# Two gathered u rows behind each batch of one-hots instead of three, the rest later

## What is computed

```python
q = (ht @ w_query).reshape(PEER_BLOCK, PEER_HEADS, PEER_QDIM)
s1 = jnp.einsum('thd,hkd->thk', q[..., :PEER_HALF], keys1)
s2 = jnp.einsum('thd,hkd->thk', q[..., PEER_HALF:], keys2)
...                                   # top 16 of the sums: expert (t, 8 heads, 16), top_s
g = jax.nn.softmax(top_s, axis=-1)
act = jax.nn.gelu(jnp.einsum('thkd,td->thk', u_tab[expert], ht))
return jnp.einsum('thk,thkd->td', g * act, v_tab[expert])
```

## Time and profile before

| | us |
|---|---|
| median of three runs | 1619.41 (1616.14 to 1623.07) |
| the profiled execution | 1620.23 |
| its span | 1618.4 |

### The profile page before, as it was taken

One profiled execution on the slowest core, in us unless ns is written; L12 is line 12 of the kernel. 1 busy time (PEld: TensorE's weight loads), 2 busy tenths in 40 slices (PEclk: granted clock), 3 DMA queues, 4 the chain that ended last, 5 costly groups with the idle time before them and its releaser, 6 DMA issues.

```text
span 1618.4 us, 21748 instructions
## 1 busy us (share of the span) xinstructions
PE 1525.7 (94%) x7951; PEld 1268.7 (78%) x7951; DVE 1269.3 (78%) x2000; ACT 688.2 (43%) x1273; POOL 996.8 (62%) x608
## 2 busy tenths in 40 slices
PE   6996997978999999999999999999999999999996
PEld 2344575437889999999999998998888888788875
DVE  6768741283889999969887897549989888999997
ACT  2030464204233433358877876344333333333332
POOL 3511000023326777776766887788978888889875
PEclk9997999989999999999999999999999999999998
DMA  9974205412306787778898999999999999999971
GB/s 367 327 216 53 30 1 186 165 52 87 122 27 206 258 277 278 269 266 326 335 361 345 355 376 346 417 333 378 376 379 362 376 376 382 383 370 383 372 267 65
DMA packets 217302, 438.91 MB, mean 271 GB/s; under 512 B 37220, under 2 KB 129892, under 8 KB 215404
## 3 DMA queue, kind: packets, MB, share of 16 engines
q1 hardware_dynamic: 179612, 302.44, 53.2%
q0 software_dynamic: 36864, 134.23, 22.6%
q10 hardware_dynamic: 720, 0.85, 0.2%
HBM read 379.66 MB, written 56.64 MB: 270 GB/s over the span
## 4 chain that ended last, share of the span: by engine, by line
PE 26%; DMA 21%; issue 8%; DVE 8%; ACT 7%; POOL 4%; SPq 2%; POOLq 0%; ACTq 0%; DVEq 0%
DMA u_raw<-in_peer_uT 9%; DMA a_in<-act_scr 7%; DMA v_raw<-in_peer_v 6%; PE ps L1649 5%; PE ps L1650 5%; PE ps L1651 5%; ACT hot1h L1582 3%; POOL vl L1541 3%; DVE ps L1745 2%; PE ps L1327 2%; PE ps L1328 2%; PE ps L1329 2%; DVE w_f L1853 2%; DVE wl L1858 1%; ACT stage L1590 1%
## 5 line engine op out<-in xcount | busy, mean ns | idle before, releaser
L1535 POOL TENSOR_TENSOR utl<-u_raw,uth 128x1024 fp32r<-128x1024 f32 x128 | 307.2, 2401 | 150.3 <-ACT uth L1554 148.9
L1649 PE MATMUL ps<-h2h,uth 128*128 128x384 f32 x1024 | 348.2, 340 | 3.1 <-POOL utl L1535 3.1
L1541 POOL TENSOR_TENSOR vl<-v_raw,vh 128x1024 fp32r<-128x1024 f32 x128 | 311.5, 2435 | 52.4 <-ACT vh L1554 50.4
L1651 PE MATMUL ps<-h2h,utl 128*128 128x384 f32 x1024 | 343.2, 335 | 0.0
L1650 PE MATMUL ps<-h2l,uth 128*128 128x384 f32 x1024 | 342.9, 335 | 0.0
L1672 PE MATMUL ps<-vh,wh 128*128 128x512 f32 x768 | 300.0, 391 | 2.8 <-DVE wl L1858 2.6
L1673 PE MATMUL ps<-vl,wh 128*128 128x512 f32 x768 | 298.9, 389 | 0.0
L1674 PE MATMUL ps<-vh,wl 128*128 128x512 f32 x768 | 298.9, 389 | 0.0
L1853 DVE TENSOR_TENSOR w_f<-a_in,g_in 128x384 f32<-128x384 f32 x128 | 213.0, 1664 | 51.7 <-DMA a_in<-act_scr 50.7
L1554 ACT ACTIVATE vh<-v_raw 128x1024 fp32r<-128x1024 f32 x128 | 135.3, 1057 | 205.9 <-DMA v_raw<-in_peer_v 165.6
L1649 PEld LDWEIGHTS ps<-h2h,uth 128*128 128x128 f32 x1024 | 192.9, 188 | 3.8 <-POOL utl L1535 3.0
(11 more groups left out here) (357 smaller groups left out, 2338.5 us busy)
## 6 DMA issues: line engine op xcount, KB each, us to landing
u_raw<-in_peer_uT SPq DMA_DIRECT2D x128, 512.0 KB
v_raw<-in_peer_v SPq DMA_DIRECT2D x128, 512.0 KB
w_ada<-in_w_ada SPq DMA_DIRECT2D x12, 2048.0 KB, 14.6
act_scr<-acts SPq DMA_DIRECT2D x64, 384.0 KB
g_scr<-stage SPq DMA_DIRECT2D x12, 2048.0 KB
g_in<-g_scr SPq DMA_DIRECT2D x32, 768.0 KB
a_in<-act_scr SPq DMA_DIRECT2D x64, 384.0 KB
w_q<-in_peer_w_query SPq DMA_DIRECT2D x8, 1024.0 KB, 5.4
```

Of the source, the lines that this page charges most:

```text
L1535: tt(k.utl[b % 3][:, :, :].rearrange(f3), k.u_raw[:, b % 4].rearrange(f3), k.uth[b % 3][:, :, :].bitcast(F32).rearrange(f3), ALU.subtract) ...
L1541: tt(k.vl[:, n % 4], k.v_raw[:, n % 4], k.vh[:, n % 4].bitcast(F32), ALU.subtract).then_inc(k.vl_done, 1)
L1649: mm(o, hi, k.h2h[:, kt, SP:T], start=(kt == 0), stop=False)
L1651: ins = mm(o, lo, k.h2h[:, kt, SP:T], start=False, stop=(kt == DK - 1))
```

## The change

Of the u rows, two instead of three follow each batch of one-hots (33 to 80), 25 instead of 23 follow behind the last batch (81 to 105), and the remaining 22 are used in v blocks 1 to 11, two in each (106 to 127). The v rows begin in v block 15 instead of 6, at six in five blocks instead of eight in seven; the last is used in v block 121 and fetched in 115. The gelu of the dots moves to v block 14. `row_steps()` moves the fetches: u rows 81 to 112 go behind u blocks 109 to 127, 113 to 127 behind v blocks 0 to 8, and the v rows begin at v block 11. No operation and no transfer is added or removed.

```diff
--- before.py
+++ after.py
@@ -1378,12 +1378,12 @@
     for j in range(2 * SLOTS):
         if j < 33:
             at = 8 + 1.3 * j
-        elif j < 105:
-            at = 53 + (j - 33) * 0.777
+        elif j < 81:
+            at = 53 + (j - 33) * 1.166
         elif j < SLOTS:
-            at = 109 + (j - 105) * 0.5
+            at = 109 + (j - 81) * 0.6
         else:
-            at = NBLK + 1 + (j - SLOTS) * 0.875
+            at = NBLK + 11 + (j - SLOTS) * 0.82
         steps[int(at)].append(j)
     return steps
 
@@ -1422,7 +1422,7 @@
         for half in range(2):
             HOT1H_AT.setdefault(block_of(PER_BATCH * m) - 2 + half, []).append((m, half))
     LAST4 = NBLK - 4
-    SP_GELU, SP_WEIGH = 4, 6
+    DOTS_END, SP_GELU, SP_WEIGH = 13, 14, 15
     f3 = "p k n -> p (k n)"
     BANK = dict(zip([(t, half) for t in range(DT) for half in range(2)], (4, 5, 6, 7, 2, 3)))
     y_sp = ps[:, 0:2].rearrange("p a n -> p (a n)")
@@ -1898,19 +1898,21 @@
         step(ins)
         for m in range(NBATCH):
             hots(m)
-            use_rows(3)
-        use_rows(SLOTS - done["rows"])
+            use_rows(2)
+        use_rows(25)
 
         weight(0)
         for n in range(1, NBLK):
             weight(n)
             split_w_low(n - 1)
-            if n == SP_WEIGH:
+            if n < DOTS_END:
+                use_rows(min(2, SLOTS - done["rows"]))
+            elif n == SP_WEIGH:
                 dve.wait_ge(k.gelu_sp, 1)
                 tt(k.w_sp[:, :], k.w_sp[:, :], k.gate_sp[:, :], ALU.mult).then_inc(k.w_sp_ready, 1)
                 dve.wait_ge(k.w_sp_ready, 1)
             if n >= SP_WEIGH:
-                use_rows(min(SLOTS, (n - SP_WEIGH + 1) * 8 // 7) + SLOTS - done["rows"])
+                use_rows(min(SLOTS, (n - SP_WEIGH + 1) * 6 // 5) + SLOTS - done["rows"])
             if n == NBLK - 3:
                 dve.wait_ge(k.row_used, 2 * SLOTS)
                 dve.wait_ge(s_gate2, 16)
```

## The result

The changed kernel takes 1635.66 us (median of 4 runs, 1632.86 to 1638.73) against 1619.48 for the kernel before (4 runs). The ratio is 1.0088, interval 1.0057 to 1.0119: 9 to 19 us slower. The forecast was 1621.5 and "within 0.5%" at 0.50. The measured time is 14 us above the forecast and outside the range that the sum gave itself (1614 to 1629). It lies inside the whole range only because that reached to rival B, which stood at 1636.

What follows compares the result with a forecast made beforehand. TensorE was taken as nearly full, DMA as the second full resource, with 18 us at most to win. Terms -7 - 3 + 5 + 7 = +2 us on 1620.2 gave 1622.2, forecast 1621.5 after allowing for the median; range 1610 to 1636.

Steps and rivals of the forecast that it cites:

- rival B: v blocks 11 to 115: DMA gives only 374 GB/s whatever is asked; +16 us, 1636; chance 0.27.
- Part 1: Beside the one-hots, 48 rows instead of 72 relieve the DMA and cut waits on `stage`: -7 us, bounds 3 and 9.4.
- Part 2: Last u blocks, 109 to 127: slightly fewer rows in 109 to 119 shorten the `u_raw` load: -3 us, bounds 0 and 6.
- Part 3: Hand-over and v blocks 0 to 8: gathers delay `a_in`, fetches slow GpSimd: +5 us, bounds 1 and 9.
- VectorE's two dots hide: v blocks 1 to 11: two dots a block cost VectorE 2.6 us but overlap its port wait behind GpSimd's `vl`.
- Rival D: v blocks 1 to 11: the dots don't hide, VectorE needs 5.2 us a block; 1630; chance 0.06.
- Part 4: v blocks 11 to 115: rows at 1.22 a block ask more than the DMA serves: +7 us, bounds 0 and 13.
- Part 5: The rest: later gelu of the dots and last v row in block 121 are covered by leads; nothing counted.
- C: v blocks: DMA can give more than the 372 GB/s asked; -10 us, 1610; chance 0.17.
- A: Whole kernel: DMA time is moved, not saved; 1621.5 us, own range 1614 to 1629; chance 0.50.

Runs made afterwards that it cites:

- e1: Kernel before with two u rows behind each batch of one-hots and the 24 freed rows left out, neither gathered nor multiplied: 1607.59 us, 0.9922 of before.
- e7: Changed kernel with the gelu of u block 127 first and the last 22 u rows left out, gather and dot: 1614.10 us, 0.9954 of before.
- e8: Changed kernel with the gelu of u block 127 first; last 22 u rows not gathered, their dots made on an old buffer: 1620.65 us, 0.9988 of before.
- e9: Kernel before with v rows from block 15 at six in five blocks and the gelu of u block 127 first: 1625.45 us, 1.0017 of before.
- e2: Changed kernel with three u rows again behind each one-hot batch, one behind the last; 22 u rows and v rows placed as changed: 1631.04 us, 1.0076 of before.
- c4: Kernel before with v rows still from block 6 but at 14 in 13 blocks, last used in block 124: 1616.91 us, 0.9983 of before.
- e4: Changed kernel with the gelu of u block 127 ahead of the high parts of v blocks 2 and 3: 1632.72 us, 1.0076 of before.
- e3: Kernel before with only its v rows moved, from block 15 at six in five blocks: 1628.43 us, 1.0051 of before.
- c1: Kernel before with v rows at 14 in 13 blocks and u rows nine before, 64 after, 22 behind the one-hots: 1638.52 us, 1.0097 of before.

## Why the prediction was right or wrong

- *The time*: the sum gave +2 us, and the kernels differ by 14 by the ratio and 16 by the medians. The upper end of the range, 1636, was 0.3 us above the measured median; that it holds the result is luck as far as the sum goes, since it was put there for rival B.
- *What bounds the kernel*: right in the main. DMA time is short from the one-hots on, and each stage moved the way the rows of that stage said. That no more than 18 us were to be won held for every version. But the 18 counted waits, and in v blocks 12 to 122 the kernel before lost 5.2 us where the waits said 2.6.
- *Part 1, -7*: right, -8.0, and -7.5 in e1. The mark (waits on `stage` of 1 to 4 us) was met with 2.4. The share fell to 0.86, not 0.80.
- *Part 2, -3*: the size was off, -1.3. The longest `u_raw` fell from 17.67 to 13.90 us, as said, and the clock held. But with rows up to the hand-over the `utl` came just in time, and TensorE waited 2.0 us for it in three waits.
- *Part 3, +5, bounds 1 and 9*: this term was mis-sized, +12.6. Its mechanism was in the text (gathers beside the hand-over, late `a_in`, waits on `wl`); e7 and e8 show that the gathers make all of it. I took 5 us more for the landing, 12.7 in all, and it took 14.9. What I left out: SP itself is held at the issue (7.22 us), so the tiles after the first come later still; the weights of blocks 2 and 3 and the last gelu hang on the second `a_in`, not the first; and the clock at 1.2 GHz behind a stop of 6.7 us costs 1.6 us more. I priced one landing and looked at one consumer. GpSimd, for which part of the 5 us stood, never made TensorE wait: none of its waits there was on `vl`.
- *"VectorE's two dots hide"*: wrong. They hide in time, since TensorE lost nothing in e8's blocks 0 to 12 beyond 0.6 us, but not in the lead: 4.41 us a block against 4.08. Rival D saw the cause, put 5.2 us on such a block, and had the wrong place for the loss; it is paid after block 12.
- *Part 4, +7*: +10.1, inside its bounds, but for another reason. The rate by itself is worth 2.1 us against before (e9) where I counted 6.4. The rest I read as lead lost before block 12 (a `w_f` begins 7.0 us ahead of that block, 12.4 before), for which my 7 held 0.6 us and the upper bound 4. The dots can take that much: e8 against e7, with the same rate, is 7.9 us by the stages and 5.5 us by the ratios (0.0034 x 1620). But they needn't: e2 has the same dots and the same v half, and loses only 3.0 us in blocks 12 to 122. It has fewer gathers ahead of the v blocks. What share of the changed kernel's lost lead is the dots' and what the late tiles' is not shown.
- *Part 5, nothing*: right, 24.6 us from block 122 to the end in every kernel.
- *The chances*: rival B had the time (1636) and 0.27. Its condition, a served rate under about 377, was just missed: 378 and 377 were served in the changed kernel and 383 in c4. So B was right in its number and its sign and not in its mechanism. C's premise held in that the DMA can give more than 376, but its sign was wrong: that doesn't help when the asking engines are late. A, the sum, had the mechanism of the first two parts and missed its own range by 7 us.
- The parts add up to +13.5 us by the stages; the spans differ by 12.7, since the u blocks of the changed kernel's execution began 0.9 us earlier.

Still open: why the first `a_in` held SP for 7.22 us. The profile names a landing of an earlier store as what ended it, but the program waits there only for the store of u blocks 0 and 1, which had long landed. Without the last 22 rows the same issue took 2.60 us (e7) and 2.29 (e8), in e4 4.10; no experiment took that apart. And whether 22 rows at one a block in the first v blocks would have kept the lead was not tried, since the v rows can't begin before all dots are done.

## What to carry to other kernels

Moving work out of a crowded stage gains only what the target stage has to spare, and the spare is counted in the lead of the buffers, not in the waits of the bottleneck engine: here 24 rows gave 8 us where they left, and cost 23 where they arrived, together with the v rows that had to begin later for them. Before blaming the longest stop of a trace, move the thing it waits for; if another wait takes its place, the cause lies further up. And look for the other direction too: spreading the v rows over seven more blocks, two lines, gained 0.2% where the whole change lost 0.9%.

## What the runs showed that I had not expected

- An engine that is 8% too slow for eleven blocks, with 0.6 us lost by TensorE there, costs 5 to 8 us in the hundred blocks after, because loads are only asked for when it frees a buffer (e8: DMA share 0.64 and 0.72; e7: 0.76 and 0.99).
- Taking the gathers away from GpSimd can slow VectorE: with `vl` back to back, four `w_f` and `wl` in a row took 2.6 us each, where before only two of the four did (e3), and it took a change in ScalarE's order to hide it (e9).
- The waits on `stage` don't fall with the rows one by one: 9.4, 8.7, 8.5 and 2.4 us with 72, 64, 60 and 48 rows.
- At 1.077 rows a v block blocks 12 to 122 take 448.8 us with no wait (c1 to c4), at 1.143 454.0 and 453.1 with waits (before, e1), and at 1.22 456.1 from a full lead (e9).
